# Gates and branch projections with tokens on partitions, a ring of five banks, and other orders on two queues

## What is computed

```
h = rms_norm(x);  P = h @ w_in          # 1792 + 1536 + 512 + 3072 columns
y_rwkv = rwkv7_time_mix(P[..., :1792])  # 8 heads x 64, delta-rule state, group norm per head, gate
y_attn = attention(P[..., 1792:3328])   # 8 heads x 64, causal, QK-norm, ALiBi
y_pool = pool_mix(P[..., 3328:3840])    # causal means over 2/4/8/16 tokens, per-group linear
branch = einsum('btnc,ncd->btnd', [y_rwkv, y_attn, y_pool], w_branch)   # 3 x (512 -> 1024)
x = x + sum_n(sigmoid(P_gate_n) * branch_n) @ w_out
x = x + square(relu(rms_norm(x) @ w_ff1)) @ w_ff2                       # 1024 -> 4096 -> 1024
```

## Time and profile before

| | |
|---|---|
| median of 3 runs | 497.85 us (497.45 to 498.67) |
| profiled execution | 497.1 us |
| its span, first to last instruction | 495.0 us |
| PE, PEld busy | 484.6 us (98%), 436.1 us (88%) |
| DVE, ACT, POOL busy | 308.2 us (62%), 239.4 us (48%), 41.6 us (8%) |
| granted TensorE clock | 1.000 throughout |
| DMA | 77.10 MB, 156 GB/s over the span |

### The profile page before, as it was taken

The page is one execution under the profiler, slowest core; times in us unless marked ns, Lnnn a source line. Parts: engine busy times, 40 slices in busy tenths (PEclk is TensorE's granted clock), DMA queues, the critical chain, the costliest instruction groups (busy, mean ns, idle before and its releaser), DMA issues.

```text
span 495.0 us, 9355 instructions
## 1 busy us (share of the span) xinstructions
PE 484.6 (98%) x3944; PEld 436.1 (88%) x3944; DVE 308.2 (62%) x454; ACT 239.4 (48%) x357; POOL 41.6 (8%) x45
## 2 busy tenths in 40 slices
PE   8999989999999999999999999999999999999997
PEld 4989976778999888899999988999999999999995
DVE  4656798865473877764328995765555555555542
ACT  6559542455552446555333354754545444454440
POOL 1000202033841011000001000000000000000000
PEclk9999999999999999999999999999999999999999
DMA  8985544454341442444224648566565566656512
GB/s 230 249 264 144 185 137 129 131 152 125 112 123 45 113 144 87 129 149 130 87 85 129 197 150 245 175 185 199 178 199 177 176 190 199 200 176 197 184 41 85
DMA packets 95800, 77.10 MB, mean 156 GB/s; under 512 B 2576, under 2 KB 85264, under 8 KB 95760
## 3 DMA queue, kind: packets, MB, share of 16 engines
q1 hardware_dynamic: 95760, 76.52, 51.6%
HBM read 75.46 MB, written 1.05 MB: 155 GB/s over the span
## 4 chain that ended last, share of the span: by engine, by line
PE 82%; DVE 7%; ACT 4%; DMA 3%; issue 2%; POOL 0%; SPq 0%; ACTq 0%
PE bank L482 24%; PE bank L483 23%; PE bank L484 23%; DMA stage<-in_w_in 3%; DVE w_lo L1095 2%; ACT w_hi L875 2%; PE bank L609 2%; PE bank L749 1%; PE bank L711 1%; PE bank L733 1%; PE bank L773 1%; DVE small L1311 1%; PE bank L784 1%; PE bank L783 1%; DVE att L1304 1%
## 5 line engine op out<-in xcount | busy, mean ns | idle before, releaser
L1095 DVE TENSOR_TENSOR w_lo<-stage,w_hi 128x1024 fp32r<-128x1024 f32 x138 | 168.6, 1229 | 120.3 <-ACT w_hi L875 120.0
L875 ACT CAST w_hi<-stage 128x1024 fp32r<-128x1024 f32 x138 | 144.1, 1052 | 120.9 <-PE bank L484 82.8
L482 PE MATMUL bank<-h_hi,w_hi 128*128 128x256 f32 x576 | 167.2, 290 | 1.4 <-DVE lmix L1350 0.6
L483 PE MATMUL bank<-h_lo,w_hi 128*128 128x256 f32 x576 | 162.8, 283 | 0.0
L484 PE MATMUL bank<-h_hi,w_lo 128*128 128x256 f32 x576 | 162.7, 283 | 0.0
L482 PEld LDWEIGHTS bank<-h_hi,w_hi 128*128 128x128 f32 x576 | 110.1, 191 | 5.5 <-issue 3.0
L483 PEld LDWEIGHTS bank<-h_lo,w_hi 128*128 128x128 f32 x576 | 110.3, 191 | 0.7
L484 PEld LDWEIGHTS bank<-h_hi,w_lo 128*128 128x128 f32 x576 | 110.2, 191 | 0.0
L482 PE MATMUL bank<-w_hi,r_hi 128*128 128x512 f32 x128 | 50.0, 391 | 0.0
L483 PE MATMUL bank<-w_lo,r_hi 128*128 128x512 f32 x128 | 50.0, 390 | 0.0
L484 PE MATMUL bank<-w_hi,r_lo 128*128 128x512 f32 x128 | 49.8, 389 | 0.0
(11 more groups left out here) (220 smaller groups left out, 644.0 us busy)
## 6 DMA issues: line engine op xcount, KB each, us to landing
stage<-in_w_ff SPq DMA_DIRECT2D x64, 512.0 KB, 4.1
stage<-in_w_in SPq DMA_DIRECT2D x54, 512.0 KB, 3.9
stage<-in_w_branch SPq DMA_DIRECT2D x12, 512.0 KB, 3.5
stage<-in_w_out SPq DMA_DIRECT2D x8, 512.0 KB, 4.3
xs<-in_x SPq DMA_DIRECT2D x2, 512.0 KB, 3.8
out<-xs SPq DMA_DIRECT2D x4, 256.0 KB, 2.1
cst<-in_consts SPq DMA_DIRECT2D x1, 768.0 KB, 6.5
att<-in_w SPq DMA_DIRECT2D x1, 256.0 KB, 4.5
```

Source lines behind the costliest of these rows:

```text
L482: pe.matmul(o, lh, rh, start=first, stop=False)
L483: pe.matmul(o, lh, rl, start=False, stop=False)
L875: nc.scalar.copy(w_hi[:, v % RING], stage[:, v % STAGES]).then_inc(hi_done, 1)
L1095: dve.tensor_tensor(w_lo[:, v % RING], stage[:, v % STAGES], w_hi[:, v % RING].bitcast(F32), ALU.subtract)\
```

## The change

Gates: the twelve feat units become six pairs of tok units of 512 columns. Each half of the tokens has a bank of its own (banks 0, 1, 2 in turn); ScalarE's two tanh come at the second unit of a pair. Branches: tokens on partitions, one bank for each half, all four pieces of the contraction in each. So the merged gates have tokens on partitions, and the output projection needs them turned: four new blocks (`turned_place`), behind parts 1 and 2 of unit 32 and parts 1 and 3 of unit 33, each four transposes on PE, a halved and rounded copy out of PSUM on ScalarE and the rest on VectorE. The splits of the second piece of unit 32 go behind its extras.

```diff
@@ units, banks and the turned merges
+UNITS += [("tok", GATES_AT + 512 * g, kh) for g in range(6) for kh in range(2)]
...
+        if t == S_HEAD:
+            ring.insert(0, 3)
+        if t == S_BR:
+            ring.remove(3)
...
+                    for tt in range(TT):
+                        use(("tok", u[1], tt), (2 * g + tt) % 3, dense=tt == 1)
...
-                    b = 2 * ((t - S_BR + 1) % 2)
-                    use(("unit", t, 0), b, dense=True)
+                    b = 2 * ((t - S_BR) % 2)
+                    use(("unit", t, 0), b)
                     use(("unit", t, 1), b + 1, dense=True)
...
+    return {(S_OUT - 1, 1): (0, 0), (S_OUT - 1, 2): (0, 1), (S_OUT, 1): (1, 0), (S_OUT, 3): (1, 1)}.get((t, p))
...
-            out += [(("pt", g, e), 2 + e) for e in range(2)]
+            out += [(("pt", g, e),) for e in range(2)]
...
-            out += [(("score", g, e), 2 + e) for e in range(2)]
+            out += [(("score", g, e),) for e in range(2)]
@@ SP: small loads
-                if v == 8:
+                if v == 14:
                     sp.dma_start(cst[:, C_BIAS:C_ALL], consts[:, C_BIAS:C_ALL]).then_inc(mask_in, 16)
-                if v == 3:
+                if v == 5:
@@ PE: a part of a branch unit, the output units, the turned merges
-                    for k in range(W // P):
-                        ins = mm3(o[:, T * i:T * i + T], wh[:, k, P * i:P * i + P], wl[:, k, P * i:P * i + P],
-                                  rh[:, k0 + k], rl[:, k0 + k], k == 0, k == W // P - 1)
+                    o = room(pe, name) if p < 2 else ps(name)
+                    for kk in range(2):
+                        k = 2 * (p // 2) + kk
+                        ins = mm3(o[:], lh[:, k0 + k, P * i:P * i + P], ll[:, k0 + k, P * i:P * i + P],
+                                  wh[:, kk], wl[:, kk], k == 0, k == 3)
+                    if p == 2:
+                        ins.then_inc(full_of(name), 1)
...
-                        if i == 0:
-                            pe.wait_ge(m_ready, 2 * u[1] + p // 2 + 1)
+                        if p < 2:
+                            copied(pe, ("mt", u[1], i))
...
+                if turned_place(t, p):
+                    ch, tt = turned_place(t, p)
+                    pe.wait_ge(m_pre, 2 * ch + tt + 1)
+                    o = room(pe, ("mt", ch, tt))
+                    for k in range(4):
+                        ins = pe.transpose(o[:, P * k:P * k + P], gates[ch][:, tt, P * k:P * k + P], ident)
+                    ins.then_inc(full_of(("mt", ch, tt)), 1)
@@ ScalarE
+                if t in S_GN and p == 3:
+                    c = S_GN.index(t)
+                    o = take(act, ("ot", c))
+                    for j in range(PAIRS):
+                        ins = nc.scalar.activation(ytmp[:, j], o[:, P * j:P * j + P], ACT.Identity, scale=col(V_LG + j),
+                                                   bias=col(V_LB + j))
+                    ins.then_inc(drained_of(("ot", c)), 1)
...
+                if turned_place(t, p):
+                    ch, tt = turned_place(t, p)
+                    o = take(act, ("mt", ch, tt))
+                    nc.scalar.mul(y_hi[:, 4 * ch:4 * ch + 4, P * tt:P * tt + P], o[:].rearrange("p (k t) -> p k t", k=4), 0.5)\
+                      .then_inc(m_hi, 1)
...
+                elif S_GATE <= t < S_BR:
+                    if u[2] == 1:
+                        for tt in range(TT):
+                            name = ("tok", u[1], tt)
+                            o = take(act, name)
+                            nc.scalar.activation(gates[(t - S_GATE) // 2][:, tt], o[:], ACT.Tanh, scale=0.5)\
+                              .then_inc(drained_of(name), 1)
@@ ScalarE and VectorE, the loop over units
-                late = t == S_FF - 1
+                late = t in (S_OUT - 1, S_FF - 1)
@@ VectorE: corner, group norm
-                            if kind == 0:
-                                dve.tensor_copy(corner.rearrange("p (i e) s -> p e i s", e=2)[:, e, 2 * g:2 * g + 2],
-                                                o[0:HD].rearrange("p (i n) -> p i n", i=2)[:, :, HD:P])
...
-                    if p == 1:
+                    if p == 2:
                         dve.wait_ge(osq_ready, c + 1)
                         link(dve.tensor_reduce(gvar, heads(osq), AX_X, ALU.add))
                         dve.tensor_scalar(gvar, gvar, 1.0 / HD, GN_EPS, ALU.mult, ALU.add).then_inc(gvar_ready, 1)
-                    if p == 2:
-                        dve.wait_ge(groot_ready, c + 1)
-                        dve.tensor_tensor(heads(oc), heads(oc), per_head(gvar), ALU.mult).then_inc(on_ready, 1)
+                if t - 1 in S_NORM and p == 1:
+                    c = S_NORM.index(t - 1)
+                    dve.wait_ge(groot_ready, c + 1)
+                    dve.tensor_tensor(o_sb, o_sb, gvar.unsqueeze(2).to_broadcast([P, HEADS, HD]), ALU.mult)\
+                       .then_inc(on_ready, 1)
@@ VectorE: the turned merges, the branches, the order of a unit
+                    dve.wait_ge(m_hi, 2 * ch + tt + 1)
+                    o = take(dve, ("mt", ch, tt))
...
+                    for tt in range(TT):
+                        copied(dve, ("tok", GATES_AT + 512 * g, tt))
+                        o = take(dve, ("unit", t, tt))
+                        dve.scalar_tensor_tensor(out=gates[g][:, tt], in0=gates[g][:, tt], scalar=1.0, in1=o[:],
+                                                 op0=ALU.add, op1=ALU.mult)\
+                           .then_inc(drained_of(("unit", t, tt)), 1)
+                        if n == 0:
+                            copied(dve, ("unit", t, tt))
+                            dve.tensor_tensor(gates[ch][:, tt], gates[ch][:, tt], gates[2 + ch][:, tt], ALU.add).then_inc(m_pre, 1)
...
+                early = t < S_VA
+                if early:
+                    extra(t, 1)
                 for v in () if late else split_places(2 * t + 1):
                     low(v)
-                extra(t, 1)
+                if not early:
+                    extra(t, 1)
```

More of the change, by code:

```diff
@@ L45 @@
 C_ID, C_BLK, C_CUM, C_BIAS = 0, 128, 256, 386
-C_SDI = C_BIAS + 384
-C_SI = C_SDI + 256
+C_SI = C_BIAS + 384
 C_LEV = C_SI + 256
@@ L120, in plan_turns @@
 def plan_turns():
-    turn, count, signalled, ring = {}, [0] * 8, [0] * 8, [0]
+    turn, count, signalled, ring = {}, [0] * 8, [0] * 8, [4, 5, 6, 7]
     def use(name, bank=None, dense=False):
         if bank is None:
-            bank = 4 + ring[0] % 4
-            ring[0] += 1
+            bank = ring[0]
+            ring.append(ring.pop(0))
         turn[name] = (bank, count[bank], signalled[bank])
@@ L149, in plan_turns @@
                     for tt in range(TT):
-                        use(("out", u[2], tt), 2 * (1 - u[2]) + tt, dense=tt == 1)
+                        use(("out", u[2], tt), 2 * u[2] + tt, dense=tt == 1)
                 elif u[0] == "ff1":
@@ L234, in dense_ends @@
         for tt in range(TT):
-            if u[0] == "branch":
-                ends[("unit", t, tt)] = 2 * t + 1 + tt
+            if u[0] == "branch" and tt == 1:
+                ends[("unit", t, 1)] = 2 * t + 2
         if u[0] == "tok" and u[2] == 1:
@@ L557, in part @@
                             pe.wait_ge(yr_ready, TT)
-                    rh, rl, k0 = {1: (y_hi, y_lo, 0), 2: (y_hi, y_lo, 4), 0: (r_hi, r_lo, 0)}[u[1]]
-                    name = ("unit", t, p // 2)
-                    o = ps(name) if i else room(pe, name)
-                    for k in range(W // P):
-                        ins = mm3(o[:, T * i:T * i + T], wh[:, k, P * i:P * i + P], wl[:, k, P * i:P * i + P],
-                                  rh[:, k0 + k], rl[:, k0 + k], k == 0, k == W // P - 1)
+                    lh, ll, k0 = {1: (y_hi, y_lo, 0), 2: (y_hi, y_lo, 4), 0: (r_hi, r_lo, 0)}[u[1]]
+                    name = ("unit", t, i)
+                    o = room(pe, name) if p < 2 else ps(name)
[5 more added lines that the diff above has]
+                        ins.then_inc(full_of(name), 1)
                 else:
@@ L717, in extra @@
                         for h in range(HEADS):
-                            ins = pe.matmul(o[HD:P, HD * h:HD * h + HD], corner[:, h], x_c[0:HD, h], start=True, stop=True)
+                            ins = pe.matmul(o[HD:P, HD * h:HD * h + HD], gm[0:HD, h, 0, HD:P], x_c[0:HD, h], start=True, stop=True)
                         ins.then_inc(full_of(("Y", c, l, 0)), 1)
@@ L1038, in finish @@
                         nc.scalar.copy(vatt[:, tt], o[:]).then_inc(drained_of(name), 1)
-                elif S_GATE <= t < S_BR:
-                    o = take(act, ("unit", t))
-                    nc.scalar.activation(gates[(t - S_GATE) // 2][:, t % 2 ^ S_GATE % 2], o[:], ACT.Tanh, scale=0.5)\
-                      .then_inc(drained_of(("unit", t)), 1)
-                elif u[0] == "branch" and u[1] == 0:
-                    for i in range(2):
-                        m = 2 * u[2] + i
```

(16 more changed lines are left out.)

48 lines of the change are left out of this document (16 added, 32 removed).

## The result

The changed kernel took **494.97 us** (median of 4, 494.27 to 496.06), the kernel before 497.99 beside it: ratio 0.9944, 95% interval 0.9922 to 0.9967. A second timing on another chip gave 494.14 against 497.20, ratio 0.9945 (0.9925 to 0.9965). The forecast was 495.3 in a range of 492.9 to 497.6, faster with a chance of 0.66. It was faster, by 3.0 us where 2.55 were forecast. The early part's term was off by 1.2 us and several others by 0.1 to 0.5, partly against each other, and the runs say which.

What follows compares the result with a forecast made beforehand. The prediction took TensorE, busy for 98% of the span, as the bound. Its terms, -2.0 - 1.9 - 3.1 + 1.7 + 0.9 + 0.25 + 1.6 = -2.55 us, set on the median 497.85, gave 495.3, range 492.9 to 497.6.

Steps and rivals of the forecast that it cites:

- Gates joined: 48 parts of 12 gate units, matmuls joined to 512 columns: 2.0 us gained, bounds nothing and 3.8.
- Branches joined: 24 nearly all quiet parts of the branch units, matmuls joined to 512 columns, 0.08 each: 1.9 us gained.
- First gate's bank: First gate unit waits 1.0 us for ScalarE's copy out of bank 0; a smaller wait behind it shrinks: 0.9 us lost.
- Four transpose blocks: Four blocks of four transposes turn the merged gates, on PE's path, 0.42 us each, no other waits: 1.7 us lost.
- Early part: Early units: later small loads and VectorE's early order remove or shorten four PE standstills; 3.1 us gained, bounds 1.0 and 3.8.
- pieces 6 and 7 come about 2 us later than otherwise, which their own lead takes: Early units: moving small loads behind piece 5 delays these weight pieces about 2 us without cost.
- early standstills stay: Rival, early units: later loads delay pieces 6 and 7, only the first standstill falls; 1.0 gained, time 497.4, chance 0.17.
- Ring of five, and VectorE's chains: Scores and gates: banks drained in time, nothing, or 1.2 us if late; five faster parts run into VectorE's chains, 0.25 lost.
- Corner block: Eight copies of 278 ns leave VectorE, PE behind none: nothing gained, up to 0.5 us if on the path.
- Group norm: Second normed half: VectorE's product comes behind two products and two weight pieces, PE waits; 1.6 us lost, bounds nothing and 2.5.
- become the bound in the branch units: Rival: VectorE takes 6.4 us a unit in units 29 to 32, PE stands at the turned merges; 499.8, chance 0.08.
- other two: Slower rivals: VectorE the bound in the branch units, 499.8, chance 0.08; joining matmuls earns nothing, 499.2, chance 0.03.

Runs made afterwards that it cites:

- gate_banks: The changed kernel with the banks of gates and branches turned round, so the first gate unit takes bank 1; stages net 0.65 us shorter up to unit 29.
- halved_branches: The changed kernel with 120 of the 144 branch matmuls of 512 columns issued as two of 256; branches took 36.46 us against 35.55.
- norm_first: The changed kernel with the second half's norm product on VectorE ahead of two weight pieces, directly behind unit 27's products; span 489.7 us against 492.1.
- corner_copies: The changed kernel with the eight corner block copies done again on VectorE, read by nothing; no PE stage from unit 8 on differs by over 0.03 us.
- best_loads_first: The changed kernel with the edits of norm_first and gate_banks, and the small loads right behind piece 2; 491.11 us, ratio 0.9877.
- loads_back: The changed kernel with the small loads behind piece 3 and masks behind piece 8 again; unit 1 to key norms 25.72 us against 26.54.
- best_loads_back: The changed kernel with the edits of norm_first, gate_banks and loads_back; median 0.8 us less than with the first two edits alone.

## Why the prediction was right, and where its terms were off

- **Gates joined**, -2.0. The 44 parts that no wait touches gave 2.2, 0.05 a part: right. Beside them two waits shrank that had not been counted: unit 16 lost 0.60 and unit 22 lost 0.48. Of the 0.60, gate_banks gave 0.38 back, which belongs to the next term but one. Both waits are marked in the trace before, 0.31 and 0.56 us, and the prediction's list of standstills stops at the four early ones:

```profile
145.99 2.00 PE L773 MATMUL bank<-lora,mat 128*128 128x64 f32 x16 [0.31 <-DVE lora L1252]
...
204.09 0.69 PE L711 MATMUL bank<-mat 64*64 64x64 f32 x32 [0.56 <-ACT mat L958]
```

- **Branches joined**, -1.9. 24 parts at 1.360 in place of 1.440: right, and halved_branches confirms 12 ns a pair. In these streams of weight load and matmul in turn, one start more costs 12 ns. The Trainium skill ("TensorE: Matmul & The Clock Gate", Back-to-back issue gap) gives the formula with 2.5 ns for an isolated matmul, which the prediction applied to a stream. For a stream of such pairs the same section gives 131 ns at 512 columns. Neither agrees with the rows, 227 ns at 512 columns and 12 ns a pair.
- **First gate's bank**, +0.9. The wait was 0.98, and 0.38 of it came off unit 16's; 0.1 had been allowed for that. Net +0.6, and gate_banks, which undid it, gained 0.65 by its stages. This is the step "a smaller wait behind it shrinks", mis-sized.
- **Four transpose blocks**, +1.7. No idle before any. 16 quiet parts would have given back 1.28 and units 29 to 36 took 0.66 more: 1.94, 0.48 a block instead of 0.42.
- **Early part**, -3.1: the term that was wrong. In the profiled execution it gave 1.86. VectorE's early order did its share at v's transposes (-1.23 of 1.34, forecast 1.1), the first standstill went (-0.78). The second (0.93) did not, and the third stayed at 0.44 where 0.3 had been left. The step that failed is "pieces 6 and 7 come about 2 us later than otherwise, which their own lead takes": the small loads slowed piece 5, which stood in front of them, to 7.4 us, piece 6 landed at 27.23, and ScalarE, whose queue is not reordered, idled 2.69, 1.11 and 2.04 us for pieces 5, 6 and 9. This is the rival "early standstills stay" for these two standstills, and not for v's. How much it costs is not one number: where the clock held, the five profiles with this early part gained 1.86, 2.23, 2.27, 2.43 and 2.92 us before v's transposes. So the profiled execution was the least lucky of them, and of the forecast's own signs, less than 2 us gained up to unit 8 shows in it alone (counted from unit 1), a standstill near 37 in four of the five. In norm_first, where no second standstill came, the term nearly held.
- **Ring of five, and VectorE's chains**, 0 and +0.25. No wait at the last score pair beyond 0.18 more in unit 21; with 0.19 in unit 20 the faster parts ran into the chains by 0.4.
- **Corner block**, 0: right (corner_copies).
- **Group norm**, +1.6: an idle of 1.25, and norm_first, which undid it, took 1.46 off the stage. It was released by VectorE's product behind two weight pieces, at 260.94. Right in place, cause and nearly in size (norm_first).
- **Start-up**, not in the sum: 0.5 us of the profiled difference. The time to the first dense matmul is 9.83 to 10.44 in the changed kernel's family and is the same code, so this is chance.

The terms as measured: -2.2 - 0.2 (the rest of unit 16) - 0.5 (unit 22) - 1.9 + 1.9 - 1.9 + 0.6 + 0.4 + 1.5 = -2.3, and with the start -2.8. The forecast -2.55 was nearer than its parts, and that is luck: an early gain 1.2 too large stood against start-up luck of 0.5 and two shrunken waits that had not been counted. Of the rivals, VectorE did not become the bound in the branch units: no idle mark stands before the turned merges. One piece of the prediction's bookkeeping is off: it gives its "other two" rivals 0.08 and 0.03 but counts 0.09 as slower, and the second of them, at 499.2, is 1.35 us from no change, inside the 1.5 that it calls the same.

## What to carry to other kernels

When TensorE is full, count starts: an inserted block, a split matmul and a moved wait each cost what the quiet rows say, to a few hundredths. What the rows don't say is how transfers share the engines; put loads that nobody waits for yet into a gap of the DMA engines (here behind piece 2, where they stood idle but for one piece), and beside pieces that have lead, since those were slowed even there (piece 3 took 6.9 us in place of 3.7). Look at the landing times of the pieces ahead of them too. A saving in front of a wait is spent in that wait, and a new wait takes from the one behind it, so cost waits in pairs.

## What the runs showed of the hardware that I had not expected

**A stretch at the lower TensorE clock in the middle of dense work.** In five of the thirteen profiles of the changed kernel and its variants the granted clock goes from 1.00 to 0.50 (1.2 GHz) between 44.4 and 45.5 us and is back before 49. gate_banks:

```profile
44.00:45.00 1.00, 1.00 (x10) 1.00 (x10) 1.00 (x2) 1.00 (x2) 0.00 (x0) 1.00 1.02 386
45.00:46.00 1.00, 1.00 (x9) 1.00 (x8) 1.00 (x2) 1.00 (x5) 0.00 (x0) 0.75 1.02 423
46.00:47.00 1.00, 1.00 (x6) 1.00 (x6) 0.76 (x2) 1.00 (x3) 0.16 (x1) 0.50 0.70 201
47.00:48.00 1.00, 1.00 (x6) 1.00 (x6) 0.69 (x1) 0.28 (x1) 1.00 (x1) 0.50 0.82 246
48.00:49.00 1.00, 1.00 (x7) 1.00 (x6) 1.00 (x3) 0.00 (x0) 1.00 (x1) 0.54 1.02 377
```

The changed kernel, whose instructions there are the same:

```profile
45.00:46.00 1.00, 1.00 (x10) 1.00 (x11) 1.00 (x2) 1.00 (x3) 0.00 (x0) 1.00 1.03 402
46.00:47.00 1.00, 1.00 (x11) 1.00 (x10) 1.00 (x2) 1.00 (x4) 0.00 (x0) 1.00 0.97 402
```

PE was busy throughout in both; ahead of it lay the standstills of the early part and the sixteen small products of the key norms. It costs 1.5 us (26.10 in place of 24.60 from the key norms to v's transposes) and goes with a part of what separates runs of one kernel. The 18 runs of the kernel before at a mean clock of 1.000 took 496.27 to 497.52, 496.83 in the mean; the 18 at 0.997 took 496.73 to 498.97, 497.73 in the mean. So small edits are better told apart by stages, or by runs of equal clock, than by medians. What sets it off was not tried.

**A transfer can be slowed by what is issued behind it, and needn't be.** Piece 5 (512 KB), with piece 4 in flight and five small loads issued right behind it, took 5.6 to 7.4 us in ten profiles, and 5.0 in best_loads_first, without these loads behind it. Piece 3, with the same five loads right behind it, took 3.9 to 4.3 us in three profiles (before, loads_back, best_loads_back), hardly more than the 3.7 to 3.9 without them. Piece 2 was in flight ahead of it for only 1.2 us, piece 4 ahead of piece 5 for 2.9 in the changed kernel, and pieces 6 and 7 were issued before piece 5 landed. Which of these makes the difference was not tried.
